# One decoder step on Trainium2: the first megabyte of input weights issued straight behind x, ahead of twelve parameter transfers

## The reference

```python
for i in range(DEPTH):                       # 2 layers
    h = rmsnorm(x, norm_g[i])                # x (288, 1024); gain norm_g (1024,)
    proj = h @ w_in[i]                       # 1024 x 9352
    qkv_a, z_a, beta, alpha, f_b, z_b, qkv_c, z_c, gates = split(proj)
    o_a = gated_deltanet(causal_conv(qkv_a, conv_a[i]), beta, alpha, a_log[i], dt_bias[i], state_dn[i])
    o_b = rwkv7(f_b, mu_b[i], w0_b[i], ..., rk_b[i], gn_g_b[i], gn_b_b[i], state_rwkv[i])
    o_c = moba_attention(qkv_c, qn_c[i], kn_c[i], paged K/V cache)
    up = einsum(stack(o_a, o_b, o_c), w_branch[i])
    x = x + sum(sigmoid(gates + b_gate[i]) * up) @ w_out[i]
    x = x + sigmoid(x @ w_pg[i] + b_pg[i]) * (ple[i] @ w_ple[i])
```

## Time and profile before

| | us |
|---|---|
| median of 3 runs | 1111.46 |
| lowest, highest | 1110.88, 1112.39 |
| the profiled execution | 1110.7 |
| its span, first to last instruction | 1109.0 |
| TensorE busy | 1084.6 (98%) |
| VectorE, ScalarE, GpSimd busy | 714.0, 335.5, 219.0 |
| mean granted TensorE clock | 0.998 of full |

### The profile page before, as it was taken

One profiled execution on the slowest core, in us unless ns is written; L12 is line 12 of the kernel. 1 busy time (PEld: TensorE's weight loads), 2 busy tenths in 40 slices (PEclk: granted clock), 3 DMA queues, 4 the chain that ended last, 5 costly groups with the idle time before them and its releaser, 6 DMA issues.

```text
span 1109.0 us, 23126 instructions
## 1 busy us (share of the span) xinstructions
PE 1084.6 (98%) x8792; PEld 874.0 (79%) x8792; DVE 714.0 (64%) x1593; ACT 335.5 (30%) x777; POOL 219.0 (20%) x399
## 2 busy tenths in 40 slices
PE   7999999999999999999999999999999999999998
PEld 5778787768778787889977788777777877887997
DVE  4675637676775675668557674667767667565856
ACT  1243222321333343210323332234223433432013
POOL 0210402020140475000001123120201206720000
PEclk9999999999999999999999999999999999999999
DMA  8733037421342798353346322555124239764331
GB/s 268 227 115 120 22 104 222 127 83 40 75 130 76 181 264 226 118 167 124 112 143 199 115 82 59 148 177 133 40 79 115 84 95 239 231 190 139 129 115 43
DMA packets 161945, 148.59 MB, mean 134 GB/s; under 512 B 43176, under 2 KB 146190, under 8 KB 161644
## 3 DMA queue, kind: packets, MB, share of 16 engines
q1 hardware_dynamic: 152084, 127.01, 39.5%
q0 software_dynamic: 7200, 16.78, 5.2%
q10 hardware_dynamic: 2552, 3.32, 1.0%
HBM read 135.42 MB, written 11.07 MB: 132 GB/s over the span
## 4 chain that ended last, share of the span: by engine, by line
PE 92%; DVE 4%; ACT 2%; issue 1%; DMA 0%; DVEq 0%; ACTq 0%; SPq 0%
PE psum L1299 48%; PE psum L1340 10%; PE psum L1361 7%; PE psum L1227 4%; PE psum L1551 2%; PE psum L1568 2%; PE psum L1415 1%; PE psum L1426 1%; PE psum L1687 1%; PE psum L1944 1%; PE psum L1902 1%; PE psum L1771 1%; PE psum L1924 1%; PE psum L1578 1%; PE psum L1460 1%
## 5 line engine op out<-in xcount | busy, mean ns | idle before, releaser
L1299 PE MATMUL psum<-x_b,ring 128*128 128x288 f32 x928 | 242.8, 411 | 0.0
L1299 PE MATMUL psum<-x_a,ring 128*128 128x288 f32 x928 | 242.7, 411 | 0.0
L1299 PEld LDWEIGHTS psum<-x_b,ring 128*128 128x128 f32 x928 | 170.1, 190 | 48.5 <-issue 6.1
L1299 PEld LDWEIGHTS psum<-x_a,ring 128*128 128x128 f32 x928 | 170.1, 190 | 48.5 <-issue 6.1
L2029 ACT ACTIVATE arena<-psum 128x512 f32<-128x512 f32 (+9 forms) x149 | 60.8, 421 | 145.2 <-PE psum L1227 52.2
L1299 PE MATMUL psum<-z,ring 128*128 128x288 f32 (+1 forms) x384 | 82.8, 368 | 0.0
L3536 POOL DMA_DIRECT2D arena<-in_cache_k x128 | 70.7, 552 | 34.6 <-issue 29.4
L1299 PEld LDWEIGHTS psum<-z,ring 128*128 128x128 f32 x384 | 62.6, 190 | 13.2 <-issue 2.3
L2029 ACT ACTIVATE arena<-arena 128x256 f32<-128x256 f32 (+9 forms) x102 | 44.6, 465 | 64.1 <-DVE arena L3283 29.9
L3420 POOL TENSOR_TENSOR triangles<-triangles,consts 128x256 f32<-128x256 f32 x30 | 22.3, 743 | 198.6 <-DVE triangles L2941 145.7
L3410 POOL TENSOR_TENSOR arena<-conv_in,params 128x128 f32<-128x128 f32 x24 | 10.6, 441 | 223.3 <-DVE conv_in L2759 175.0
(11 more groups left out here) (482 smaller groups left out, 2055.0 us busy)
## 6 DMA issues: line engine op xcount, KB each, us to landing
ring<-in_w_in SPq DMA_DIRECT2D x72, 1024.0 KB, 5.4
ring<-in_w_branch SPq DMA_DIRECT2D x12, 1024.0 KB, 5.2
arena<-in_cache_k POOLq DMA_DIRECT2D x128, 64.0 KB, 5.3
arena<-in_cache_v SPq DMA_DIRECT2D x32, 256.0 KB, 5.7
ring<-in_w_out SPq DMA_DIRECT2D x8, 1024.0 KB, 5.0
ring<-in_w_pg SPq DMA_DIRECT2D x8, 1024.0 KB, 5.0
arena<-in_state_dn SPq DMA_DIRECT2D x8, 512.0 KB, 7.3
out_dn_sample<-arena POOLq DMA_DIRECT2D x8, 512.0 KB, 6.3
```

What stands on the lines that cost most here:

```text
L1299: ins = mm(out[:, 0:n], lhs, rhs(k), start=k == 0, stop=k == k_tiles - 1)
```

## The change

SP issues ring part 0 straight behind x_sample, and the twelve parameter transfers behind it; the other three parts stay where they were. No wait, size or destination is changed, and no other engine's program.

```diff
@@ -1112,8 +1112,9 @@
                     sp.dma_start(XN[:, 1, :], A["x_prompt"][0, 128:256, :]).then_inc(S.sem("x1_loaded"), 16)
                 else:
                     sp.dma_start(XN[0:32, 2, :], A["x_sample"].rearrange("s t d -> (s t) d")).then_inc(S.sem("x1_loaded"), 16)
+                    load_chunk()
                     param_rows(sp, 0, PROWS[7:])
-                    for c in range(RING):
+                    for c in range(1, RING):
                         load_chunk()
                         if c == 2:
                             sp.dma_start(CN[:, 263:], A["const_table"][:, 263:]).then_inc(S.sem("tables_loaded"), 16)
```

## The result

Over 22 runs of each kernel on the same chips the changed kernel's median is 1113.15 us against 1111.68 us before: a ratio of 1.0016, 95% interval 1.0009 to 1.0022, so 1.0 to 2.4 us longer. The interval excludes no change at all. The ratio lies inside the 0.2% that the prediction called no change; the upper end of the interval lies just outside it. The profiled execution took 1113.77 us with a span of 1112.1 us.

A forecast was written before the change was run, and what follows sets the result against it. TensorE, busy in 98% of the span, was taken to bound the kernel. A later start of +1.0 and clock of -0.15 gave +0.85: 1111.6 on the profiled 1110.7, 1112.3 us against the median; range 1110.4 to 1113.6.

The forecast's parts named there:

- (a): SP's queue: part 0, issued at 2.83 instead of 6.75, lands at 9.5 instead of 12.05, 2.5 us sooner.
- (b): Twelve small transfers behind part 0: closings of about 0.2 us each, 2.4 us, rows complete at 11.9, between 9.6 and 12.3.
- (c): Parameter transposes to first product: 1.2 us, so the first weight matmul starts at 13.1 against 12.08, 1.0 us later.
- the -0.5 that is named with the chances: Lower end of the forecast's +0.9 from the bounds of (b), which run to +1.4; chance 0.79.
- (d): TensorE's clock, low until 16.2 as before: 3.1 us of matmuls fall into it rather than 3.4, so 0.15 us comes back.
- The rival of a second low stretch: TensorE runs slow from 13.1 to 19.6: +1.0 + 1.55, 1114.0 us, slower; chance 0.09.
- (e): Sum of squares, a_log's use, second part, tables and later loads: nothing else is late, cost nothing.
- Overlapping closings, the fast rival: Rows land at 9.8, first matmul at 11.05: 1110.5 with the clock falling (chance 0.04), 1108.8 with it held (0.08).
- The signs: Expected in the profile: new 2 us TensorE hole, transposes near 11.9, first weight matmul near 13.1, later rows shifted by one constant.

The follow-up runs named there:

- e2: The changed kernel with part 0 behind five of the twelve parameter transfers and ahead of the other seven: 1113.12 us, ratio 1.0016 to the kernel before.
- e7: The kernel before with eight more 64-byte transfers, read by nothing, on ScalarE's queue behind its seven rows: 1112.64 us, ratio 1.0007.
- e4: The kernel before with three matmuls on constants that nobody reads, between the parameter transposes and the first weight matmul: 1111.59 us, ratio 1.0003.
- e8: The changed kernel profiled again without an edit: 1113.47 us, ratio 1.0018 to the kernel before.
- e9: The kernel before with qn_c and kn_c each loaded by one transfer with a repeated source instead of two: 1112.48 us, ratio 1.0004.
- e10: The changed kernel with qn_c and kn_c each loaded by one transfer with a repeated source instead of two: 1113.49 us, ratio 1.0016 to the kernel before.
- e6: The kernel before with norm_g on its own semaphore and transpose, the other rows transposed behind the first twelve weight matmuls: 1112.03 us, ratio 1.0001.

## Why the prediction was right

The time, 1112.3 forecast and 1113.15 measured, and the class, no change that can be told by 0.2%, came out as said, for the reason given: the rows take the part's place as the last to come. The size was low, +0.85 against +1.5 between the medians. That it came so near is in part luck: two errors of the sum cancel ((a) and (b)), and in the pair of profiles on which the sum was built the span moved by 3.1 us. By its steps:

- **(a) Part 0 in front.** Forecast 9.5, measured 10.5. The near end was the wrong one: I let a megabyte move alone at 381 GB/s from 6.0, while from 6 to 9 us the engines carried 242 to 349 GB/s. The other way of counting, from the landings of the earlier trace rows, gave 10.2. x_sample also came 0.7 us later, but so it did before in its second profile (7.6), and TensorE had time to spare.
- **(b) Twelve closings.** Forecast 2.4 us, measured 1.85, by 0.15 each. The bounds, 0 to 2.8 us behind x_sample, held: in the kernel before the rows were complete at 9.33, 2.4 us behind it. As a mechanism the step was half told. Rows that wait for the part ahead of them in the queue are what the changed kernel shows, by the pause from 8.38 to 9.96; the earlier trace rows, which the prediction read for this, have two large parts and no small transfer. What it didn't see is that small transfers take time of an engine ahead of the part too: e2 and e7 show the part later by that. The two errors of (a) and (b) partly cancel: rows at 12.36 for 11.9. One bound was taken wrongly: rows at 9.6 with the 1.2 us of (c) give a first matmul at 10.8, 1.3 us sooner, and not the -0.5 that is named with the chances; the range, from 1110.4, has about -1.1.
- **(c) From rows to matmul.** Forecast 1.2 us and a first matmul at 13.1, measured 1.4 and 13.81. I counted to the end of the first product and left out what lies between it and the matmul: the products begin at 13.29 at 0.29 each, the first is done near 13.6, and the matmul starts 0.2 later. With 0.5 from the rows this makes the forecast's +1.0 into +1.7.
- **(d) The clock.** Forecast -0.15, measured +1.02 in the profile and +0.3 as a mean of five profiles against five. This is the step that failed in sign. It took the let-up at 16.2 as fixed; by the trace's clock records it came anywhere from 14.4 us (e4) to 20.2 (e8), and later on average where the first weight matmul was later (18.5 for 16.8). The rival of a second low stretch is what the profiled execution shows, priced at +1.55 and measured at +1.02 beside a start that was later than forecast. The medians, 1.5 us apart, didn't follow it to its 1114.0.
- **(e) Nothing else late.** Right. The sum of squares ended before 19 us and was used at 22.45, and the waits after 30 us kept their lengths.
- **Overlapping closings, the fast rival.** Excluded by 12.36, where it had 9.8, and by the rows' distance behind the part, which grows with their number (1.22 us with seven, 1.85 with twelve).
- **The signs.** The hole ahead of the parameter transposes, the wait for VectorE and the constant shift came. Part 0 landed 7.7 us after its issue for 6.5 to 7, a_log was issued at 7.31 for 6.9, and the engines carried 242 GB/s from 6 to 7 us for over 300.

What stays open: the second group of 24 begins 2.75 us later than before in the one pair of profiles and 3.0 in the other (23.49 for 20.49), which is more than the medians show. In the second pair the spans are only 2.0 us apart (1111.8 and 1109.8): a microsecond comes back at 249, 321 and 675 us, in steps of 0.2 to 0.4 us, in stretches that the change doesn't touch. Two pairs can't tell luck with the clock from something that only profiled executions do.

## What to carry to other kernels

Before a large load is moved ahead of small ones, ask who waits for the small ones and what stands behind that wait: here a matmul needed both, but 1.5 us of transposes, a copy and a product stood behind the rows and nothing behind the weights, so the rows had to land first. Count small transfers as work on a DMA engine, here 0.15 to 0.20 us each, that a large transfer in flight may have to wait for as well; ahead of part 0 twelve of them cost it nothing that e9 could show, and eight more cost 1.2 us (e7). And when the trace shows a wait of 1.2 us for a load, look how close the next wait is: here x itself was next, and not even the version without the rows on its path gained anything measurable.

## What the runs showed of the hardware

- **One slow share holds a megabyte.** In e7 fifteen sixteenths of part 0 were complete at 11.90 and the last at 13.20, behind eight transfers of 64 bytes. The eight came from ScalarE's queue and the part from SP's. In e2, with three rows of four partitions among the five transfers ahead of it, part 0 has twelve shares complete by 9.95 and four from 10.78 to 11.10. The last three increments of the rows in the changed kernel are at 12.01, 12.18 and 12.36, one every 0.17 us, and the last five in the kernel before 0.18 to 0.21 us apart.
- **Small transfers wait behind a large one in their queue.** Behind part 0 in SP's queue the rows' increments stop for 1.0 to 2.0 us and go on within 0.3 us of part 0's first share, in six profiles of six.
- **A transfer with a repeated source is slow to issue.** 0.76 and 0.56 us, in e9 and again in e10, where a plain one of half the size took about 0.27 (two in 0.55, in the kernel before).
- **The clock column is blind before its first record.** Until then the profile prints full clock, whatever the speed. In e2, stretches as above:

```profile
14.00:15.00 1.00, 1.00 (x3) 0.71 (x4) 1.00 (x4) 0.17 (x1) 0.00 (x0) 1.00 1.08 429
15.00:16.00 1.00, 1.00 (x4) 0.71 (x3) 0.97 (x6) 0.00 (x0) 0.00 (x0) 1.00 1.01 418
...
18.00:19.00 1.00, 1.00 (x6) 0.79 (x5) 0.82 (x2) 0.00 (x0) 0.00 (x0) 1.00 1.12 295
```

The clock column says 1.00 in all three, yet TensorE gets through 3 or 4 records in a microsecond up to 16, as in the changed kernel's stretches at 0.50, and 6 at 18. So the 1.00 at 5.5 and 7.0 us in the earlier trace rows stands ahead of the first record (9.4 us) and tells nothing of the speed there. Of the thirteen profiles, three (before, changed and e6) reached full clock near 9.1 to 9.8 us, lost it again near 12.5 to 13.2, and got through the transposes of x sooner (the last 16 in 2.42 us in the changed kernel and 2.69 in e6, all 24 in 4.66 before). The other ten needed 2.95 or 2.96 us for the 16, or 5.02 for all 24, and had no full clock before 14.4. That the clock fell after the hole, as the prediction read it, describes the three; in the ten there was nothing to fall from, and the first weight matmuls ran slowly all the same. The count of records in a stretch is the safer reading.
